# MLP up products as seven block products of 256 columns, MLP down products as two halves of 256 columns

## What is computed

```python
def squared_relu_mlp(h, w_up, w_down):
    return jnp.square(jax.nn.relu(h @ w_up)) @ w_down

for layer in range(DEPTH):            # DEPTH = 2
    h = rms_norm(x, mix_norm[layer])
    x = x + mixer(h, ...)             # gated delta rule in layer 0, sparse attention in layer 1
    x = x + squared_relu_mlp(rms_norm(x, mlp_norm[layer]), w_up[layer], w_down[layer])
```

## Time and profile before

| | before |
|---|---|
| median of three runs | 2100.04 us |
| span of the profiled execution | 2099.7 us |
| TensorE matmuls | 2076.6 us busy (99%), 11148 |
| TensorE weight loads | 1645.5 us busy (78%), 11148 |
| VectorE | 947.6 us busy (45%) |
| ScalarE | 933.3 us busy (44%) |
| GpSimd | 759.2 us busy (36%) |

### The profile page before, as it was taken

One profiled execution on the slowest core, in us unless ns is written; L12 is line 12 of the kernel. 1 busy time (PEld: TensorE's weight loads), 2 busy tenths in 40 slices (PEclk: granted clock), 3 DMA queues, 4 the chain that ended last, 5 costly groups with the idle time before them and its releaser, 6 DMA issues.

```text
span 2099.7 us, 28844 instructions
## 1 busy us (share of the span) xinstructions
PE 2076.6 (99%) x11148; PEld 1645.5 (78%) x11148; DVE 947.6 (45%) x1431; ACT 933.3 (44%) x1477; POOL 759.2 (36%) x316
## 2 busy tenths in 40 slices
...
GB/s 155 134 123 70 45 104 99 92 101 91 94 99 88 146 96 31 2 14 92 100 91 101 91 101 101 74 97 81 12 81 90 91 93 94 85 22 61 91 100 81
DMA packets 62710, 178.96 MB, mean 85 GB/s; under 512 B 17776, under 2 KB 18160, under 8 KB 62592
## 3 DMA queue, kind: packets, MB, share of 16 engines
...
...
## 4 chain that ended last, share of the span: by engine, by line
issue 48%; PE 34%; POOL 16%; ACT 1%; POOLq 0%; DMA 0%; SPq 0%; DVE 0%
POOL w_lo L2709 16%; PE banks L760 9%; PE banks L762 9%; PE banks L761 9%; PE banks L1282 1%; PE banks L1295 1%; PE banks L1267 1%; PE banks L811 1%; PE banks L1273 1%; PE banks L1239 0%; DMA x<-in_x 0%; PE banks L1330 0%; POOLq L2715 0%; POOLq L2717 0%; PE banks L1331 0%
## 5 line engine op out<-in xcount | busy, mean ns | idle before, releaser
L2709 POOL TENSOR_TENSOR w_lo<-raw,w_hi 128x1024 fp32r<-128x1024 f32 (+1 forms) x312 | 759.0, 2434 | 1322.8 <-ACT w_hi L1415 1322.7
L760 PE MATMUL banks<-h_lo,w_hi 128*128 128x512 f32 (+1 forms) x1408 | 567.0, 403 | 9.3 <-POOL w_lo L2709 9.3
L762 PE MATMUL banks<-h_hi,w_hi 128*128 128x512 f32 (+1 forms) x1408 | 554.7, 394 | 0.0
L761 PE MATMUL banks<-h_hi,w_lo 128*128 128x512 f32 (+1 forms) x1408 | 551.5, 392 | 0.0
L1415 ACT ACTIVATE w_hi<-raw 128x1024 fp32r<-128x1024 f32 (+1 forms) x312 | 327.9, 1051 | 489.4 <-PE banks L762 456.5
L760 PEld LDWEIGHTS banks<-h_lo,w_hi 128*128 128x128 f32 (+1 forms) x1408 | 264.4, 188 | 73.8 <-POOL w_lo L2709 8.7
L761 PEld LDWEIGHTS banks<-h_hi,w_lo 128*128 128x128 f32 (+1 forms) x1408 | 264.5, 188 | 62.2 <-issue 4.8
L762 PEld LDWEIGHTS banks<-h_hi,w_hi 128*128 128x128 f32 (+1 forms) x1408 | 264.3, 188 | 60.7 <-issue 0.7
L760 PE MATMUL banks<-a_lo,w_hi 128*128 128x512 f32 x768 | 304.5, 397 | 0.0
L762 PE MATMUL banks<-a_hi,w_hi 128*128 128x512 f32 x768 | 301.6, 393 | 0.0
L761 PE MATMUL banks<-a_hi,w_lo 128*128 128x512 f32 x768 | 299.8, 390 | 0.0
...
## 6 DMA issues: line engine op xcount, KB each, us to landing
raw<-in_weights SPq DMA_DIRECT2D x311, 512.0 KB, 3.6
...
```

The costliest lines, as they stand in the source:

```text
L760: mm(out, w_hi, x_lo, start=first, stop=False)
L761: mm(out, w_lo, x_hi, start=False, stop=False)
L762: return mm(out, w_hi, x_hi, start=False, stop=last)
L2709: return nc.gpsimd.tensor_tensor(c.w_lo[:, slot, 0:n], c.raw[:, slot, 0:n], c.w_hi[:, slot, 0:n].bitcast(F32), ALU.subtract)
```

## The change

Up products. Weights and activations are taken as blocks of two by two: an output pair (two tiles of 128 features) times 512 tokens, the inner pair of tiles likewise, and the tokens in two halves of 256. Instead of eight block products seven are made, of sums and differences of the blocks (`SEVEN`), and the four output blocks are put together from them. One group `g` (two output tiles) takes two weight blocks, with 7 x 2 x 3 = 42 matmuls of 256 columns each, 84 for the group, where two `gemm` calls made 48 of 512 columns. Four groups make an up stage. The seven outputs lie in four PSUM banks, groups alternate between the two sets of four.

For this,
- VectorE makes three sums of weight blocks and one auxiliary for each up block (`weight_sums`: four additions of 128 x 256, both operands in SBUF). It does so three blocks ahead: in group `g` for the second block of group `g + 1` before it reads the group's products, and for the first block of group `g + 2` among them; for the first three blocks of a stage in the stage before. ScalarE waits for the sums (`c.weight_sums`) and rounds 768 columns more (`w_hi_s`), GpSimd makes 768 columns more (`low_sums`).
- VectorE makes four sums of each pair of activation tiles (`input_sums`) in the stage ahead of the MLP, and splits them.
- In each group ScalarE copies the first product out of PSUM (`c.first`); VectorE makes seven additions of 256 columns, and ReLU now reads and writes `c.relu` in SBUF (`rectified`).
- ScalarE squares and rounds group `g - 1` after the rounding of the first block of group `g + 1`, and copies the first product of group `g` after the rounding of the second.

Down products (`gemm_halves`) are the same products and sums, each of the three matmuls of a tile made for tokens 0 to 255 and then for 256 to 511: 48 matmuls of 256 columns for a block instead of 24 of 512. The loops of SyncE and GpSimd over the weight blocks are written out.

```diff
+PAIRS = KT // 2
+W_S1, W_11, W_12, W_22, W_S2, W_S3, W_S4 = range(7)
+X_11, X_21, X_22, X_T1, X_T2, X_T3, X_T4 = range(7)
+SEVEN = [("p1", W_11, X_11), ("p2", W_12, X_21), ("p6", W_S2, X_T2), ("p3", W_S4, X_22), ("p7", W_S3, X_T3),
+         ("p5", W_S1, X_T1), ("p4", W_22, X_T4)]
...
+    def gemm_halves(key, x_hi, x_lo, needs=None):
+        out = claim(key)
+        pe.wait_ge(c.w_lo_ready, block[key][0] + 1)
+        slot = block[key][0] % RING
+        for k in range(KT):
+            if needs:
+                needs(k)
+            w_hi, w_lo = [t[:, slot, k * P:k * P + P] for t in (c.w_hi, c.w_lo)]
+            for half in range(2):
+                t = slice(half * HALF, half * HALF + HALF)
+                mm(out[:, t], w_hi, x_lo[k][:, t], start=k == half == 0, stop=False, skip_group_check=True)
+                mm(out[:, t], w_lo, x_hi[k][:, t], start=False, stop=False, skip_group_check=True)
+                ins = mm(out[:, t], w_hi, x_hi[k][:, t], start=False, stop=k == KT - 1, skip_group_check=True)
+        ins.then_inc(c.block_used, 1)
     def token_major(keys, x_hi, x_lo, n_in, needs=None, beside=None):
...
+    def seven(layer, q, g, half, first):
+        b = block[("up", layer, q, g)][0] + half
+        pe.wait_ge(c.w_lo_ready, b + 1)
+        for n, (name, w, x) in enumerate(SEVEN):
+            key = ("up", layer, q, g, name)
+            bnk, hi, lo, at = bank[key][0], *weight_block(w)
+            if half == 0 and n % 2 == 0:
+                pe.wait_ge(c.bank_read[bnk], beside[("up", layer, q, g, bnk)])
+            out = c.psum[bnk][:, n % 2 * HALF:n % 2 * HALF + HALF]
+            for k in range(2):
+                i, cols = 2 * half + k, slice(at + k * P, at + k * P + P)
+                if first:
+                    pe.wait_ge(c.split_lo, split[("ht" if x >= X_T1 else "hx", 2 * layer + 1, i)] + 1)
+                w_hi, w_lo, x_hi, x_lo = hi[:, b % RING, cols], lo[:, b % RING, cols], c.hs_hi[:, i, x, :], c.hs_lo[:, i, x, :]
+                mm(out, w_hi, x_lo, start=half == k == n % 2 == 0, stop=False, skip_group_check=True)
+                mm(out, w_lo, x_hi, start=False, stop=False, skip_group_check=True)
+                ins = mm(out, w_hi, x_hi, start=False, stop=half == k == 1, skip_group_check=True)
+            if n == len(SEVEN) - 1:
+                ins.then_inc(c.block_used, 1)
+            elif half and n % 2:
+                ins.then_inc(c.bank_filled[bnk], 1)
     def mlp(layer):
         n = 2 * layer + 1
         for q in range(FF_PARTS):
+            for g in range(PAIRS):
+                seven(layer, q, g, 0, q == g == 0)
+                if q == g == 0:
+                    norm_sum(n)
+                seven(layer, q, g, 1, q == g == 0)
             for m in range(KT):
-                gemm(("up", layer, q, m), h_hi, h_lo, needs=parted("h", n) if q == m == 0 else None)
-                if q == m == 0:
-                    norm_sum(n)
-            for m in range(KT):
-                gemm(("down", layer, q, m), a_hi, a_lo, needs=parted("a", layer, q) if m == 0 else None)
+                gemm_halves(("down", layer, q, m), a_hi, a_lo, needs=parted("a", layer, q) if m == 0 else None)
     gemm(("ab",), h_hi, h_lo, needs=parted("h", 0), width=AB_ROWS)
...
+            if b in sums:
+                act.wait_ge(c.weight_sums, sums.index(b) + 1)
+                f(c.w_hi_s[:, b % RING, :], c.raw_s[:, b % RING, :], ACT.Copy)
             f(c.w_hi[:, b % RING, 0:n], c.raw[:, b % RING, 0:n], ACT.Copy).then_inc(c.w_hi_ready, 1)
             count["w"] += 1
...
+    def pair_hi(n, k):
+        x_final(act, c, bank, n, k)
+        i, gain = k // 2, norm_gain(c, pa, n, k)
+        if k % 2:
+            f(c.hs_hi[:, i, X_21:X_22 + 1, :].rearrange("p b t -> p (b t)"), c.x[:, k, :], ACT.Copy, scale=gain).then_inc(c.split_hi, 1)
+        else:
+            f(c.hs_hi[:, i, X_11, :], c.x[:, k, 0:HALF], ACT.Copy, scale=gain)
+        norm_square(n, k)
+    def sums_hi(n, i):
+        act.wait_ge(c.t_ready, (n // 2) * PAIRS + i + 1)
+        f(c.hs_hi[:, i, X_T1:X_T4 + 1, :].rearrange("p b t -> p (b t)"), c.t_sum[:, :, :].rearrange("p b t -> p (b t)"), ACT.Copy)\
+            .then_inc(c.split_hi, 1)
...
     def mlp(layer):
-        weights(block[("up", layer, 0, 0)][1] + 2)
+        weights(block[("up", layer, 0, 0)][0] + 2)
         norm_root(2 * layer + 1)
+        def squared(q, g):
+            for m in (2 * g, 2 * g + 1):
+                key = ("a", layer, q, m)
+                act.wait_ge(c.relu_ready, (layer * FF_PARTS + q) * KT + m + 1)
+                act.wait_ge(c.split_lo, split[key] - 2)
+                step(f(c.stage[:, split[key] % 3, :], c.relu[:, m % 2, :], ACT.Square))
+                hi(key, c.a_hi[:, m, :])
         for q in range(FF_PARTS):
-            for m in range(KT):
-                up, key, i = ("up", layer, q, m), ("a", layer, q, m), (layer * FF_PARTS + q) * KT + m
-                passed(*up)
-                read(up)
-                act.wait_ge(c.split_lo, split[key] - 2)
-                step(f(c.stage[:, split[key] % 3, :], c.relu[:, i % 2, :], ACT.Square))
-                hi(key, c.a_hi[:, m, :])
+            for g in range(PAIRS):
+                key = ("up", layer, q, g, "p1")
+                weights(block[key[:4]][0] + 2)
+                if g:
+                    squared(q, g - 1)
+                weights(block[key[:4]][0] + 3)
+                f(c.first[:, g % 2, :], filled((*key[:4], "p2"))[:, 0:HALF], ACT.Copy).then_inc(release(key), 1)
+            squared(q, PAIRS - 1)
             if q < FF_PARTS - 1:
                 for m in range(KT):
                     passed("down", layer, q, m)
...
+    def weight_sums(b):
+        slot = b % RING
+        part = [c.raw[:, slot, n * SUM_BLOCK:(n + 1) * SUM_BLOCK] for n in range(4)]
+        part += [c.raw_s[:, slot, n * SUM_BLOCK:(n + 1) * SUM_BLOCK] for n in range(3)]
+        dve.wait_ge(c.raw_loaded[slot], 16 * (b // RING + 1))
+        tt_op(part[W_S3], part[W_11], part[W_S1], ALU.subtract)
+        s1 = marked(tt_op(part[W_S1], part[W_S1], part[W_22], ALU.add))
+        yield
+        after(s1)
+        s2 = marked(tt_op(part[W_S2], part[W_S1], part[W_11], ALU.subtract))
+        yield
+        after(s2)
+        tt_op(part[W_S4], part[W_12], part[W_S2], ALU.subtract).then_inc(c.weight_sums, 1)
+        yield
...
+    def input_sums(n, i):
+        g1, g2 = [norm_gain(c, pa, n, 2 * i + s) for s in range(2)]
+        x1, x2, t = c.x[:, 2 * i, :], c.x[:, 2 * i + 1, :], c.t_sum
+        x_final(dve, c, bank, n, 2 * i)
+        x_final(dve, c, bank, n, 2 * i + 1)
+        if n == 3 or i:
+            dve.wait_ge(c.split_lo, split[("ht", n, i - 1)] + 1 if i else split[("ht", 1, PAIRS - 1)] + 1)
+        v.tensor_scalar(c.part[:, 0, :], x1[:, 0:HALF], g1, None, ALU.mult)
+        gained = marked(v.tensor_scalar(c.part[:, 1, :], x1[:, HALF:T], g1, None, ALU.mult))
+        after(gained)
+        t1 = marked(tt_op(t[:, 0, :], c.part[:, 1, :], c.part[:, 0, :], ALU.subtract))
+        stt(t[:, 2, :], x2[:, HALF:T], g2, c.part[:, 1, :], ALU.mult, ALU.subtract)
+        after(t1)
+        t2 = marked(stt(t[:, 1, :], x2[:, HALF:T], g2, t[:, 0, :], ALU.mult, ALU.subtract))
+        after(t2)
+        stt(t[:, 3, :], x2[:, 0:HALF], g2, t[:, 1, :], ALU.mult, ALU.subtract).then_inc(c.t_ready, 1)
+    def pair_lo(n, i):
+        dve.wait_ge(c.split_hi, split[("hx", n, i)] + 1)
+        for k, src, rows in ((2 * i, c.x[:, 2 * i, 0:HALF], slice(X_11, X_11 + 1)), (2 * i + 1, c.x[:, 2 * i + 1, :], slice(X_21, X_22 + 1))):
+            hi_part, lo_part = [t[:, i, rows, :].rearrange("p b t -> p (b t)") for t in (c.hs_hi, c.hs_lo)]
+            ins = stt(lo_part, src, norm_gain(c, pa, n, k), hi_part.bitcast(F32), ALU.mult, ALU.subtract)
+        ins.then_inc(c.split_lo, 1)
+    def sums_lo(n, i):
+        dve.wait_ge(c.split_hi, split[("ht", n, i)] + 1)
+        tt_op(c.hs_lo[:, i, X_T1:X_T4 + 1, :], c.t_sum[:, :, :], c.hs_hi[:, i, X_T1:X_T4 + 1, :].bitcast(F32), ALU.subtract)\
+            .then_inc(c.split_lo, 1)
+    def sums_before_pairs(n, *key):
+        first = block[("up", n // 2, 0, 0)][0]
+        last = block[(*key, KT - 1)][1]
+        for m in range(KT):
+            add_to_x((*key, m), m)
+            if m:
+                norm_add(n, m)
+            if m % 2:
+                input_sums(n, m // 2)
+            if m % 2 == 0 and m:
+                pair_lo(n, m // 2 - 1)
+                sums_lo(n, m // 2 - 1)
+            b = block[(*key, m)][1] + RING
+            if b >= first and (m == KT - 1 or block[(*key, m + 1)][1] + RING > b):
+                all_sums(b)
+        norm_add(n, KT)
+        pair_lo(n, PAIRS - 1)
+        sums_lo(n, PAIRS - 1)
     def mlp(layer, next_norm):
         r = root(2 * layer + 1)
+        def low(q, m):
+            lo(("a", layer, q, m), c.a_hi[:, m, :], c.a_lo[:, m, :])
...
+        def rectified(m):
+            y = c.relu[:, m % 2, :]
```

(58 more changed lines are left out.)

97 lines of the change are left out of this document (75 added, 22 removed).

## The result

The changed kernel takes 2267.8 us (median of four runs, 2261.2 to 2271.2) where the kernel before, run beside it, takes 2099.9 (four runs): 1.0795 times as long, with a 95% interval of 1.077 to 1.082. The forecast was 2311 us, with a range of 2175 to 2405.

The account below looks back on a forecast made before the run. TensorE, busy for 99% of the span, was taken as the bound. 2100 + 148 (up stages) + 37 (ahead of the MLPs) + 26 (down stages) = 2311 us, range 2175 to 2405.

Parts of the forecast that it names:

- the ring: Up stages: serial waits through ScalarE, VectorE and GpSimd from one first block's weight sums to the next; 19.2 us, TensorE outside.
- holds: Up stages: two-SBUF-operand VectorE operations and GpSimd operations delay each other when one starts inside the other; 14.6 us a group.
- 65 to 70% TensorE: Sign of being right: TensorE busy for that share of up stages, which GpSimd's `w_lo` ends.
- rival (2): Up stages: idle gaps lower TensorE's clock to 1.2 GHz, about 12 us a stage, +96, total 2407 us; chance 0.14.
- The pieces' maxima: Sign of being right: longest 256-column weight-sum additions on VectorE near 2.3 to 2.9 us, mean well over 0.42.
- 18.1 + hand-overs = 19.2 us: Up stages: the ring's steps sum to 18.1 us, with some 15 hand-overs at 0.07 us 19.2.
- the layout: One up stage laid out by hand: last `w_lo` at 55.9 us, TensorE ends 61.1, down stage waits 1.3 for last `a_lo`.
- 148 us forecast: Up stages: 62.4 us instead of 43.95, +18.5 each, eight times +148.
- rival (1): Up stages: holds cost nothing, ring 15.3 us, a stage about 48, total 2178 us; chance 0.15.
- 3072 x 123 ns, +26: Down stages: 3072 matmuls of 256 columns at 123 ns, 377.9 us against 351.6, +26 us.
- Entries, +37: Ahead of each MLP: VectorE's extra sums delay the first groups, +24 in layer 0, +12 in layer 1, together +37.
- Rival (3): Faster: a 256-column matmul costs 112 ns and the ring is hidden, entries 0, total 2042 us; chance 0.05.

Follow-up runs that it names:

- one-operand runs: Changed kernel with VectorE's weight-sum additions (1.0591), these plus squares before rounding (1.0318), or all two-operand VectorE work in up stages (1.0293) made one-operand maxima.
- the run with the squares first: Changed kernel with a group's squares taken before ScalarE rounds weights of later blocks; 2198.5 us, ratio 1.0493.
- the first experiment: Changed kernel with the MLP down products whole again (512 columns), up products left as seven; 2252.1 us, ratio 1.0745.
- the run with pieces of one operand: Changed kernel with the 256-column weight-sum additions replaced by maxima of one SBUF operand, apart from each layer's first three blocks; 2221.1 us, ratio 1.0591.
- all covers off: Changed kernel without two-operand VectorE work in up stages, low sums or input sums, with squares before rounding and whole down products; 2098.7 us, ratio 1.0018.

## Why the prediction was right, and where it was off

**Direction and cause: right.** The time went the way that was forecast, and the ring with its holds is what the profile and the one-operand runs show. An up stage was predicted at 65 to 70% TensorE, ended by `w_lo`; it was ended by `w_lo` (96.3 of 116.7 us), but busy for 44.05/56.47 = 78%. At 118 ns its 336 matmuls would be 39.6 us, 70%: most of the rest is some 30 matmuls at the lower clock, a sign of rival (2). The pieces' maxima were put at 2.3 to 2.9 us; the timeline has 2.56.

**The ring, step "18.1 + hand-overs = 19.2 us": 1.65 too long.** By the timeline above: ScalarE 442.03 to 445.00, 2.97 (put at 3.12); `a_lo` and the hold to GpSimd's end at 448.49, with the hand-over, 3.49 (3.09); pieces and `a_lo` to 450.50, 2.01 (2.36); ScalarE with hand-over 1.91 (1.86); GpSimd with hand-over to 456.65, 4.24 (4.22); VectorE to 459.46, 2.81 (3.48); the last hand-over 0.12. The error is mostly in the hand-overs, with 0.35 us shown of the 1.05 that I had put, and in VectorE's last steps, 0.67 too long. I added recorded durations, 0.42 and 0.69 us, but operations that don't need each other's result start 0.33 and 0.61 apart (529.97 and 530.30, 529.36 and 529.97, in the rows of the run with the squares first). Of the fifteen hand-overs only four show. Over a stage that makes 4.6 us: the low half of the last block came at 51.3 us where the layout had 55.9, in which the last part of the ring also had 1.15 us of hand-overs, more than the whole ring's 1.05. This term, 148 us forecast and 100 measured, is the miss: 48 us too much, of which 5 were made up elsewhere: 0.5 in the down stages, 2 outside the MLPs, and 2.4 by which the medians differ more than the profiled spans.

**The holds, for which rival (1) gave 2178: real.** The three kernels with one-operand work take 43 us off for the pieces alone, and 105 for all, with the order unchanged. The order is worth 63 us alone and 57 more on top of the pieces (1.0591 to 1.0318). Both sides of the step were right: each step of the order waits, and the two engines shut each other out on top.

**Down stages, "3072 x 123 ns, +26": right by two errors.** Measured +27, but 123 ns was too much, at 113 and mostly 118; the halves cost 1.2 us a stage. A further 2.3 us a stage stays with whole products, most of it TensorE waiting for the last `a_lo` (L846, 14.3 us in all). I had counted that wait, as 1.3 us, in the up stage. That the two errors cancel is luck. The whole products of the first experiment, which take away the price and keep the wait, separate the two. The formula that the prediction takes from the Trainium skill's "TensorE: Matmul & The Clock Gate", section "Back-to-back issue gap", is given there for a single matmul by itself and not for a stream of loads and matmuls. So its 109 ns was no figure for this stream.

**Entries, +37: right in size.** The entries and their up stages cost 62 us, less two times 12.5 for the ring 37; the split is 22 and 15, where I said 24 and 12. The place was wrong: I had let the first half group of layer 0 run and its second half wait until 323, when VectorE is done. VectorE was done at 323.5, and the second half did start then, but most of the wait, 20.4 us, came ahead of the first product, for a bank.

**The clock, rival (2): half true.** It did fall in the up stages, to 0.94 and in two of layer 1 to 0.91, behind gaps of 3.5 and 4.5 us from one start to the next. By the timeline this is covered: the matmuls after the first such gap ended at 455.0, and the low half for the next ones at 454.28 + 2.37 = 456.65. The stages bear this out: the two at 0.91 took 56.48 and 56.37 us, the four at 0.94 from 56.39 to 56.47. Once the ring was shortened elsewhere, in the run without low sums, slow matmuls turned up at the head of a down stage, where nothing covers them. The rival's mechanism was right and its place wrong; filling the gaps neither raised the clock nor moved the time, so it prices nothing. The price where nothing covers it can be read from the run with pieces of one operand: its five down stages with a granted clock of 0.965 took 48.9 to 49.0 us, the three at 1.00 from 47.4 to 47.5, some 1.5 us for 16 slow matmuls.

**Rival (3), faster:** its point of decision was a ring under 9.4 us. With all covers off the ring was at last hidden, and the time still only reached that of the kernel before: a product cost 116.3 ns and more, not 112, and the entries cost 28 us, not nothing.
